# The sample tokens as the first tile of the band layer's pair pipeline, its output keys and values turned inside it, and a bias table written to memory in two steps

## What is computed

```python
a_p, b_p, c_p, xq_p, g_p = in_proj(xp, ln_g[l], w_in[l])      # prompt
a_s, b_s, c_s, xq_s, g_s = in_proj(xs, ln_g[l], w_in[l])      # sample
o_p = band_attn_prompt(q, k_p, v_p, rel_bias_table[j])   # own chunk of 64 + 8 chunks before
# sample: 12 heads of 64; each sequence sees its 128 cached keys and its 16 new ones
kk = concatenate([k_cache, k]); vv = concatenate([v_cache, v])
s = einsum('bqhd,bkhd->bhqk', q, kk) * 64 ** -0.5 + rel_bias_lookup(table, dist)
o_s = einsum('bhqk,bkhd->bqhd', softmax(s), vv)
# both: cross-attention of 4 heads into 256 memory tokens (cached ones for the sample)
y = concatenate([mix_o, cross_attn(xq, mk, mv)]) * silu(gate)
x = x + y @ w_out[l]
# outputs too: the newest 512 rows of k_p and v_p, and k_s, v_s of all 128 sample tokens
```

## Time and profile before

| what | us |
|---|---|
| median of 3 runs | 3077.28 (3074.36 to 3078.67) |
| the profiled execution | 3073.57 |
| its span, first to last instruction | 3072.1 |
| `begin`, to the first product of `project` | 0 to 138.3 |
| `project` of layer 0, to its last product | 138.3 to 795.9 |
| `keys_out`, `sample_band`, `sample_cross` | 803.7 to 956.2 |
| `prompt_band` | 956.2 to about 1598 |
| layer 1 | about 1602 to the end |

### The profile page before, as it was taken

One profiled execution on the slowest core, in us unless ns is written; L12 is line 12 of the kernel. 1 busy time (PEld: TensorE's weight loads), 2 busy tenths in 40 slices (PEclk: granted clock), 3 DMA queues, 4 the chain that ended last, 5 costly groups with the idle time before them and its releaser, 6 DMA issues. The chain is left out here.

```text
span 3072.1 us, 46241 instructions
## 1 busy us (share of the span) xinstructions
PE 2722.0 (89%) x17237; PEld 2333.5 (76%) x17237; DVE 1222.4 (40%) x2559; ACT 914.2 (30%) x2116; POOL 272.2 (9%) x469
## 2 busy tenths in 40 slices
PE   2799999999477999999977999999995688898886
PEld 1499999999454677777756999999995577787775
DVE  1401100122144555555545013101215677777773
ACT  1411111111024555555534122111110434434342
POOL 1100000000001211111112000000001111111111
PEclk6899999999788999999998999999998899999998
DMA  7521221211535422222214123221215432333331
GB/s 125 169 74 62 74 74 62 73 61 63 171 122 170 114 65 76 62 68 74 77 64 140 64 86 120 92 73 62 74 47 174 120 86 87 88 86 91 91 84 40
DMA packets 250077, 277.15 MB, mean 90 GB/s; under 512 B 13092, under 2 KB 203868, under 8 KB 249916
## 3 DMA queue, kind: packets, MB, share of 16 engines
q1 hardware_dynamic: 236924, 225.58, 24.3%
q0 software_dynamic: 12880, 49.42, 4.6%
q10 hardware_dynamic: 112, 0.04, 0.0%
HBM read 174.85 MB, written 100.14 MB: 90 GB/s over the span
## 5 line engine op out<-in xcount | busy, mean ns | idle before, releaser
L709 PE MATMUL pj_acc<-xh,pj_wh 128*128 128x384 f32 (+1 forms) x2240 | 800.2, 357 | 11.0 <-DVE pj_wl L671 11.0
L709 PE MATMUL pj_acc<-xl,pj_wh 128*128 128x384 f32 (+1 forms) x2240 | 801.0, 358 | 0.0
L709 PE MATMUL pj_acc<-xh,pj_wl 128*128 128x384 f32 (+1 forms) x2240 | 800.5, 357 | 0.0
L709 PEld LDWEIGHTS pj_acc<-xh,pj_wh 128*128 128x128 f32 x2240 | 421.6, 188 | 47.6 <-DVE pj_wl L671 11.5
L709 PEld LDWEIGHTS pj_acc<-xh,pj_wl 128*128 128x128 f32 x2240 | 421.4, 188 | 36.3
L709 PEld LDWEIGHTS pj_acc<-xl,pj_wh 128*128 128x128 f32 x2240 | 421.2, 188 | 35.4
L671 DVE TENSOR_TENSOR pj_wl<-pj_wg,pj_wh 128x1024 fp32r<-128x1024 f32 x56 | 68.6, 1225 | 723.8 <-ACT pj_wh L638 723.8
L648 ACT ACTIVATE pj_stg<-pj_acc 128x384 f32<-128x384 f32 (+1 forms) x170 | 90.8, 534 | 673.4 <-PE pj_acc L709 673.4
L2089 PE MATMUL pr_SC<-pr_q,pr_k 128*128 128x128 f32 x1536 | 196.6, 283 | 58.7 <-DVE pr_q L2224 23.8
L2089 PEld LDWEIGHTS pr_SC<-pr_q,pr_k 128*128 128x128 f32 x1536 | 186.6, 197 | 70.5 <-DVE pr_q L2224 21.6
L1691 ACT COPY pb_pt<-pb_TP 128x384 f32<-128x384 f32 (+2 forms) x256 | 101.1, 395 | 280.7 <-PE pb_TP L1517 212.1
(11 more groups left out here) (278 smaller groups left out, 3838.9 us busy)
## 6 DMA issues: line engine op xcount, KB each, us to landing
proj<-pj_stg SPq DMA_DIRECT2D x168, 192.0 KB, 1.9
proj<-pj_stg SPq DMA_DIRECT2D x112, 256.0 KB, 2.0
pj_wraw<-in_w_in_dram POOLq DMA_DIRECT2D x26, 1024.0 KB, 6.1
pb_gate<-proj SPq DMA_DIRECT2D x17, 512.0 KB, 5.0
x_mid<-pb_x POOLq DMA_DIRECT2D x17, 512.0 KB, 3.0
nt_x<-x_mid SPq DMA_DIRECT2D x17, 512.0 KB, 4.4
pr_x<-x_mid SPq DMA_DIRECT2D x17, 512.0 KB, 3.4
pr_gate<-proj SPq DMA_DIRECT2D x17, 512.0 KB, 4.3
```

Of the source, the lines that this page charges most:

```text
L709: ins = nc.tensor.matmul(acc[b][:, 0:n], w[p][:, k], x[:, k, at:at + n], start=(k == 0 and x is xh and w is wh), stop=(k == KD - 1 and x i ...
```

## The change

- **The bias table.** `begin` now writes the 12 rows once, to `ext_row` (36 KB). ACT issues the 128-fold copy from `ext_row` to `ext` at the start of `project`, right after it has split the first weights; SP waits for it at the end of `project`.
- **The stages.** `keys_out`, `sample_band` and, for layer 0, `sample_cross` and `SplitOutWeights` are gone. `prompt_band` has 17 tiles (136 units): tile 0 is the sample, with the two cross pairs first and then the six band pairs.
- **Tile 0.** For each pair, PE turns the cached keys of eight sequences into `OP` in rounds of four transposes (four rounds for a cross pair, two for a band pair); DVE and ACT take the rounds in turn, and a round waits for the copy of the one before. The queries are cut into four quads of 32 (two sequences each). Loads of the cached keys and values are cut by pair, in runs of 512 bytes, and go to spare places of the ring buffers.
- **The projection** runs one tile later: job T-1 beside tile T, so none lies beside tile 0. `w_out` is loaded and split during tile 0: one chunk after pairs 2 to 5, two after pairs 6 and 7.
- **The outputs.** The values of the last four prompt tiles and of the sample are stored from the ring `vring`; their keys are turned by six transposes each, the sample's before unit 0, the prompt's four between quarters of the last projection.
- **The prompt's bias** comes in two loads, columns 512 to 640 during tile 0, the rest at the start of tile 1, with POOL's memsets behind them.

```diff
+    def widen(self, eng, ext, ext_row):
+        eng.wait_ge(self.s_row, 16)
+        eng.dma_start(ext, ext_row.unsqueeze(1).to_broadcast([HA, P, 768])).then_inc(self.s_ext, 16)
...
-                        sp.dma_start(ext, extv[:].unsqueeze(1).to_broadcast([HA, P, 768])).then_inc(s_ext, 16)
+                        sp.dma_start(ext_row, extv[:]).then_inc(s_row, 16)
...
                 high(0, 0)
+                if keep:
+                    keep.widen(act, ext, ext_row)
...
+        if l == 0:
+            with Semaphores(nc, software) as sem:
+                prompt_band(nc, l, sem, sb_in, ps_in, v)
+            return
...
-            with ExitStack() as inner:
-                if l == 0:
-                    band = band_loads(sem_l, sb_in(inner), v)
-                    keys_out(nc, sem_l, sb_in, ps_in, v["ident"], v["proj"], v["a_k_prompt"], v["a_v_prompt"],
-                             v["a_k_sample"], v["a_v_sample"], band)
-                    sample_band(nc, sem_l, sb_in, ps_in, v, o_s, band, cross)
-                else:
-                    sample_hgrn(nc, sem_l, sb_in, ps_in, v, o_s, cross)
...
+        KEYS = [own, late, [own[0]], [late[0]], [vspare[:, 0]], [own[0]], [late[0]], [vspare[:, 1]]]
+        VALS = [[vspare[:, 0], vspare[:, 1]], [vspare[:, 2], kspare], [own[1]], [late[1]], [vspare[:, 1]], [own[1]], [late[1]],
+                [vspare[:, 2]]]
...
+        def rounds(p):
+            return 4 if p < XP else 2
...
+        def chunks(p):
+            return {2: (0,), 3: (1,), 4: (2,), 5: (3,), 6: (4, 5), 7: (6, 7)}.get(p, ())
...
+                load_queries(0)
+                load_pair(0)
+                load_pair(1)
+                load_values(0)
+                load_keys(0)
+                sp.wait_ge(s_big, 1)
+                for b in range(SB):
+                    rows = slice(b * SL, (b + 1) * SL)
+                    half = slice(b % 2 * P, (b % 2 + 1) * P)
+                    new = slice(2 * P + b * SL, 2 * P + (b + 1) * SL)
+                    sp.dma_start(bias[rows, :, half], bass.AP(v["ext"].tensor, 511, [[767, SL], [P * 768, HA], [1, P]])
+                                 ).then_inc(s_sb, 16)
+                    sp.dma_start(bias[rows, :, new], bass.AP(v["ext"].tensor, 639, [[767, SL], [P * 768, HA], [1, SL]])
+                                 ).then_inc(s_sb, 16)
+                load_gate(0)
+                sp.wait_ge(s_kt, rounds_before(1))
+                load_pair(2)
+                load_weights(0)
+                sp.wait_ge(s_kt, rounds_before(2))
+                load_pair(3)
+                load_weights(1)
+                sp.wait_ge(s_pv, 1)
+                load_pair(4)
+                load_weights(2)
+                load_weights(3)
+                sp.wait_ge(s_pv, 3)
+                load_pair(5)
+                band_bias(slice(512, BAND), s_pb1)
+                load_weights(4)
+                load_weights(5)
+                sp.wait_ge(s_pv, 4)
+                load_pair(6)
+                store_values(0)
+                sp.wait_ge(s_tka, 1)
+                sp.wait_ge(s_tkd, 1)
+                sp.dma_start(v["a_k_sample"][0].rearrange("b s h d -> (b s) (h d)"), tT[:].rearrange("p g n -> p (g n)")
+                             ).then_inc(s_ko, 16)
+                load_weights(6)
+                load_weights(7)
+                sp.wait_ge(s_pv, 5)
+                load_pair(7)
+                sp.wait_ge(s_ko, 16)
+                load_values(1)
+                load_queries(1)
+                load_keys(1)
+                load_gate(1)
+                load_x(0)
+                load_x(1)
+                for T in range(2, TILES):
+                    sp.wait_ge(s_sc, 2 * PAIRS * (T - 1))
+                    load_queries(T)
+                    load_values(T)
+                    if T > RING:
+                        sp.wait_ge(s_sc, 2 * (PAIRS * (T - 1) + MG))
+                    load_keys(T)
+                    if T == 2:
+                        sp.wait_ge(s_min, 2 * PAIRS)
+                        band_bias(slice(0, 512), s_pb2)
...
+                store_values(NT)
+                for i in range(4):
+                    sp.wait_ge(s_tka, i + 2)
+                    sp.wait_ge(s_tkd, i + 2)
...
+                sp.wait_ge(s_vo, 16 * 5)
+                sp.wait_ge(s_ko, 16 * 5)
...
+                nc.gpsimd.memset(bias[:, :, 0:SWIDE], BIG).then_inc(s_big, 1)
...
+                    if T == 0 and p == 5:
+                        pool.wait_ge(s_pb1, 16)
+                        pool.wait_ge(s_gr, u + 1)
+                        nc.gpsimd.memset(bias[0:64, :, BAND - CHUNK:], BIG).then_inc(s_bias, 1)
+                        pool.wait_ge(s_bias, 1)
+                    if T == 1 and p == 3:
+                        pool.wait_ge(s_pb2, 16)
+                        pool.wait_ge(s_gr, u + 1)
+                        nc.gpsimd.memset(bias[64:P, :, 0:CHUNK], BIG).then_inc(s_bias, 1)
+                        pool.wait_ge(s_bias, 2)
...
+                def keys_turn(p):
+                    for r in range(rounds(p)):
+                        n = rounds_before(p) + r
+                        if r == 0:
+                            pe.wait_ge(s_raw[p], 16 * len(KEYS[p]))
+                        if n:
+                            pe.wait_ge((s_ked if n % 2 == 0 else s_kea), (n + 1) // 2)
...
+                        ins.then_inc(s_kt, 1)
...
+                def scores_sample(u, p):
+                    done = rounds_before(p + 1)
+                    pe.wait_ge(s_kea, (done + 1) // 2)
+                    pe.wait_ge(s_ked, done // 2)
+                    wait(pe, s_min, 2 * u)
+                    for qd in range(QUADS):
+                        rows = slice(QR * qd, QR * (qd + 1))
+                        for h in range(2):
+                            po = HD * h
+                            if p < XP:
+                                ins = nc.tensor.matmul(SC[h][rows, 0:512], xq[0][po:po + HD, p, rows],
+                                                       kring[po:po + HD, qd, P:RING * P], start=True, stop=True)
+                                if qd == QUADS - 1:
+                                    ins.then_inc(s_sc, 1)
+                            else:
+                                nc.tensor.matmul(SC[h][rows, 0:2 * P], q[0][po:po + HD, p - XP, rows],
+                                                 kring[po:po + HD, qd, 2 * P:4 * P], start=True, stop=True)
+                    if p >= XP:
+                        if p == XP:
+                            pe.wait_ge(s_ldk[0], 16)
+                        for h in range(2):
+                            po = HD * h
+                            nc.tensor.matmul(SC[h][:, 2 * P:3 * P], q[0][po:po + HD, p - XP], kring[po:po + HD, p - XP, 0:P],
+                                             start=True, stop=True).then_inc(s_sc, 1)
...
+                def values_sample(p):
+                    slot = p % 4 * P
+                    pe.wait_ge(s_val[p], 16 * (len(VALS[p]) + (1 if p == 1 else 0)))
+                    if p >= XP:
+                        for h in range(2):
+                            c = (p - XP) * P + h * HD
+                            nc.tensor.matmul(OB[HD * h:HD * h + HD, slot:slot + P], vring[:, 0, c:c + HD], pt[h][:, 2 * P:3 * P],
+                                             start=True, stop=False)
+                    n = 4 if p < XP else 2
+                    for qd in range(QUADS):
+                        at = qd * QR
+                        for i in range(n):
...
+                            for h in range(2):
+                                ins = nc.tensor.matmul(OB[HD * h:HD * h + HD, slot + at:slot + at + QR], src[:, h * HD:(h + 1) * HD],
+                                                       pt[h][:, i * P + at:i * P + at + QR],
+                                                       start=(p < XP and i == 0),
+                                                       stop=(i == n - 1 and (p < XP or qd == QUADS - 1)))
+                    return ins
...
+                        if job == 0 and n == 0:
+                            pe.wait_ge(s_wl, KD)
...
+                keys_turn(0)
                 scores(0)
-                pe.wait_ge(s_y, 2)
                 turn_values(0)
+                turn_keys(0, 0)
                 for u in range(U_ALL):
                     turn(u, 0)
-                    project(t, 6 * p, 6 * p + 2)
+                    if T:
+                        project(T - 1, 6 * p, 6 * p + 2)
+                    elif p + 1 < PAIRS:
+                        keys_turn(p + 1)
                     if u + 1 < U_ALL:
                         scores(u + 1)
                     turn(u, 1)
-                    project(t, 6 * p + 2, 6 * p + 6)
-                    if p == MG and t + 1 < NT:
-                        turn_values(t + 1)
+                    if T:
+                        project(T - 1, 6 * p + 2, 6 * p + 6)
```

(27 more changed lines are left out.)

518 lines of the change are left out of this document (281 added, 237 removed).

## The result

The changed kernel takes 2961.97 us (median of 4 runs, 2955.35 to 2971.68) against 3077.07 before: a ratio of 0.9629, 95% interval 0.9599 to 0.9660. The prediction was 2952, range 2930 to 2985. The profiled execution took 2955.35 us, 1.5 more than its span; it is the fastest of the four, 6.6 under the median. Forecast for it were 2948.6.

The account below looks back on a forecast made before the run. PE bounds most of the kernel, except a load stall in `begin` and sample stages that each fill and drain. Terms -53 (table), -75 (sample tile) and +3 (end) sum to -125: 2952 us on the median, range 2930 to 2985.

Parts of the forecast that it names:

- The table: In `begin`, writing 36 KB instead of 4.7 MB removes PE's 54.9 us stall: -53 us, bounds -46 and -55.
- I give back 2 us: In `begin`, tiles loaded during the stall would now come at the loads' own pace, costing 2 us of the gain.
- The copy: The 128-fold DRAM to DRAM copy at the start of `project` costs 0; the other end was 24 us.
- The 36 us of cover: In `project`, POOL's weights for group 2 land at 145.7 us and are needed by 181.8.
- rival B: The copy starves `project` of its weights: +24 us, 2976 us; chance 0.08.
- The sample tile: Tile 0 brings PE to the first projection at 895 us, not 969.9: -75 us, bounds -90 and -55.
- The chain: A band pair's dependent steps in tile 0, from turning keys to value products, bound it: 6.8 us, 6.9 with weight splitting.
- I add 0.1: In tile 0, splitting one `w_out` chunk falls mostly in the chain's value part, adding 0.1 us to a band pair.
- Rival A: PE works at half clock through tile 0: 16 us over six band pairs, 2968 us; chance 0.18.
- C: The table wasn't what held `begin`; loads stay slow and the -53 stays away: 3005 us; chance 0.04.
- D: Tile 0's 512-byte cache runs move no faster than the table's write, 70 GB/s: +55 us, 3132 us; chance 0.02.
- The end: Four times six key transposes join the last projection, with DVE's copies ahead of an add: +3 us, bounds +1 and +5.

Follow-up runs that it names:

- `two_banks`: Changed kernel with the rounds of transposed keys alternating between `OP` and an idle half of a scores bank: 2944.09 us, ratio 0.9562.
- `write_on_act`: Kernel before, with the 4.7 MB table write issued on ACT's queue at 13.5 us, not SP's at 17.4: 3062.69 us (one run).
- `more_sems`: Changed kernel with 38 more semaphores in `prompt_band` that nobody uses: 2957.54 us (one run).

## Why the prediction was right, and where it was off

**The total** was off by 6.7 us in the profiled execution (2948.6 against 2955.35) and by 10 in the median, inside the range. Part of that closeness is luck, since the errors of the terms cancel: `begin` 6.6 in my favour, sample tile 6.1 and the end 3.2 against, layer 1 and `project` 4.0 that no edit made.

**The table, -53, measured -59.6, outside my bounds (-46 to -55).** The stall of 54.9 was read rightly. The step that failed is "I give back 2 us": behind the stall no gain from ready loads shows; PE went on at a clock of 0.92, was busy 3.6 us longer and waited 1.3 more. And the mechanism was only half named: the order of the queue is 17 us of it, the slow source 42.

**The copy, 0, measured 0 in time.** I allowed it 67 us from the nearest row; it moved 288 GB/s from 79 to 85 us, and its last packets are at 99.4, 23 us behind its issue at 76.3. It did hinder: the weights that POOL loads beside it took 11.4 us to land, the median is 6.1. The 36 us of cover held, and rival B never came near.

**The sample tile, -75, measured -68.9.** Two readings of rows were loose and did no harm: the even part of the earlier trace rows spans 270 to 319 GB/s and not 283 to 303 (its mean is the 290 used), and group 2 starts at 185.1 by the 23.4 us of a group. The chain (keys, scores, minimum, exp, transposes, values) and its price of 6.9 us a pair were right for four of five pairs, and not by luck: in pair 3 the two rounds of keys took 3.15 us (3.1) and the scores 1.0 (1.2). The term that was mis-sized is the splitting of the weights: "I add 0.1" where PE waits 3.8 us in pair 6, because two chunks stand ahead of a copy that PE needs at once. I had asked what of the split lies beside PE's work, and not what is queued behind it on DVE. Two more terms of this pair, 1.9 us together, I had left out: the wait for pair 7's keys and the six transposes of the next tile's values. Pair 0, at half clock, took 15.7 and not 13; pair 7 took 7.5 and not 10; the first transposes of scores came 2.1 us later than forecast.

**Rival A** was more than a rival: it is a state in which some executions of this kernel run. The chance of 0.18 was put on "the kernel is so", where the question was how often. Its price, 16 us, lies between what two traces show (13.4 and 16.9). **C and D** did not occur: the table was the cause, and tile 0, most of whose loads are runs of 512 bytes, moved 242 GB/s up to 784 us and 245 from there to 830.

**The end, +3, measured +6.2.** The transposes are the +3 (3.2). The other 3.0 stood in no row but in the code: a stage's semaphores are cleared one after another while all engines wait. I had counted the DMAs and instructions of the change and not its semaphores.

**What stays open:** why the clock falls in one execution and not in another of the same code; whether this is the changed kernel's spread, since the kernel before, without the tile, spread by up to 20 us; why pair 0's clock came back earlier in `two_banks`, and what its other 11 us in the median are; what of the 3.8 us in pair 6 comes back with less splitting there; and what holds the copy at 290 GB/s with 16 engines.

## What to carry to other kernels

Ask of a transfer that blocks others what its engines do per packet, before moving it to another queue: twelve partitions as the source cost three times as much as DRAM, and a small row written once and spread from DRAM removed the stall. Where PE waits for short hand-overs all the time, look at the granted clock in traces of several executions before explaining a few microseconds; here a second bank for the round trip took 18 us off the median and idle work in the gaps 12, more than either's trace accounts for. Before an engine gets more work in a slot, list what is queued behind it there, and count what a stage holds, semaphores too.

## What the runs showed of the hardware

- A 3 KB packet took a DMA engine 406 ns when its source was one of 12 partitions (`write_on_act`), 131 ns from DRAM with 12 engines and 168 ns with 16; from 79 to 85 us the last two come to the same 290 GB/s.
- The same code in the sample tile: band pairs 6.8 us apart at a clock of 0.96, or 10.1 us at 0.58 and 0.57, from one execution to the next. With the gaps filled, 1.00 in the one trace there is.
- 38 more semaphores in a stage put off the next one by 2.7 us, 71 ns each (`more_sems`).
